# A two-block transformer kernel on one core: five small moves in the order of loads, weight splits and bank emptying

## The reference, cut to what matters

```python
g = jax.nn.sigmoid(gates.reshape(b, s, N_BRANCH, D_MODEL))
merged = g[:, :, 0] * (o_fox @ w_fox_out) + g[:, :, 1] * (o_dsa @ w_dsa_out) + g[:, :, 2] * (o_sb @ w_sb_out)
return merged @ w_out
```

## Time and profile before

| | us |
|---|---|
| median of 3 runs | 2405.51 (2404.97 to 2410.62) |
| profiled execution | 2403.74 |
| its span | 2401.9 |
| TensorE busy | 2264.0 (94%) |
| VectorE busy | 1502.5 (63%) |
| ScalarE busy | 1081.5 (45%) |
| GpSimd busy | 350.4 (15%) |
| mean granted TensorE clock | 0.968 |

### The profile page before, as it was taken

How to read it: one execution, slowest core, us unless ns; L and a number is a source line. 1 busy time by engine, 2 the same in 40 slices (tenths; PEclk the granted TensorE clock), 3 DMA queues, 4 the chain that set the end, 5 groups by cost and what they waited for, 6 DMA issues and landing times.

```text
span 2401.9 us, 40464 instructions
## 1 busy us (share of the span) xinstructions
PE 2264.0 (94%) x17516; PEld 2157.3 (90%) x17516; DVE 1502.5 (63%) x2186; ACT 1081.5 (45%) x1285; POOL 350.4 (15%) x300
## 2 busy tenths in 40 slices
PE   7988899998789999999999899999999999899998
PEld 6878799997679999999998798999999988788998
DVE  5566687843467878667756547667656556556665
ACT  4445544534455445335336355335334236445333
POOL 1680000045000000000535110000000015310000
PEclk9999999998899999999999799999999999989999
DMA  8663255543234554555643344455555643344552
GB/s 244 178 169 105 97 178 200 161 157 106 70 106 168 181 196 159 194 175 175 186 127 109 113 162 155 162 201 173 186 177 176 161 146 108 106 158 132 181 203 91
DMA packets 314660, 374.28 MB, mean 156 GB/s; under 512 B 23127, under 2 KB 280931, under 8 KB 313331
## 3 DMA queue, kind: packets, MB, share of 16 engines
q1 hardware_dynamic: 309283, 353.83, 45.5%
q0 software_dynamic: 3424, 11.50, 1.7%
q10 hardware_dynamic: 1776, 6.37, 0.8%
HBM read 362.49 MB, written 9.18 MB: 155 GB/s over the span
## 4 chain that ended last, share of the span: by engine, by line
PE 83%; DVE 9%; ACT 5%; issue 2%; POOL 0%; DMA 0%; ACTq 0%; DVEq 0%
PE banks L857 23%; PE banks L860 22%; PE banks L858 22%; PE banks L885 3%; PE banks L886 3%; PE banks L889 3%; DVE wlo L1752 2%; ACT whi L1335 2%; PE banks L1113 1%; PE banks L1151 1%; PE banks L1137 1%; PE banks L1033 1%; PE banks L1020 1%; DVE x_lo L1810 1%; PE banks L867 1%
## 5 line engine op out<-in xcount | busy, mean ns | idle before, releaser
L857 PE MATMUL banks<-x_hi,wlo 128*128 128x256 f32 (+1 forms) x4344 | 1110.0, 288 | 39.7 <-DVE wlo L1752 15.4
L858 PE MATMUL banks<-x_lo,whi 128*128 128x256 f32 (+1 forms) x4344 | 1098.5, 285 | 0.0
L1335 ACT ACTIVATE whi<-raw 128x2048 fp32r<-128x2048 f32 (+1 forms) x340 | 637.3, 1878 | 680.0 <-PE banks L860 617.6
L857 PEld LDWEIGHTS banks<-x_hi,wlo 128*128 128x128 f32 (+1 forms) x4344 | 843.6, 194 | 60.5 <-issue 34.2
L858 PEld LDWEIGHTS banks<-x_lo,whi 128*128 128x128 f32 (+1 forms) x4344 | 844.5, 194 | 1.0 <-issue 1.0
L1752 DVE TENSOR_TENSOR wlo<-raw,whi 128x2048 fp32r<-128x2048 f32 (+2 forms) x292 | 658.3, 2264 | 170.7 <-ACT whi L1335 170.4
L860 PE MATMUL banks<-x_hi,whi 128*128 128x256 f32 x4344 | 691.9, 285 | 0.0
L860 PEld LDWEIGHTS banks<-x_hi,whi 128*128 128x128 f32 x4344 | 599.6, 194 | 3.6 <-issue 0.9
L825 POOL TENSOR_TENSOR wlo<-raw,whi 128x512 fp32r<-128x512 f32 x184 | 239.7, 1340 | 1173.9 <-ACT whi L1335 1173.9
L885 PE MATMUL banks<-x_hi,wlo 128*128 128x256 f32 (+1 forms) x632 | 177.1, 312 | 31.5 <-DVE gt L1786 11.6
L886 PE MATMUL banks<-x_lo,whi 128*128 128x256 f32 (+1 forms) x632 | 169.1, 299 | 0.0
(11 more groups left out here) (254 smaller groups left out, 1966.3 us busy)
## 6 DMA issues: line engine op xcount, KB each, us to landing
raw<-in_ffn_w_gu SPq DMA_DIRECT2D x88, 1024.0 KB, 5.2
raw<-in_ffn_w_down SPq DMA_DIRECT2D x66, 1024.0 KB, 5.1
raw<-in_ffn_w_up SPq DMA_DIRECT2D x44, 1024.0 KB, 5.1
raw<-in_w_in SPq DMA_DIRECT2D x42, 1024.0 KB, 5.3
raw<-in_ca_w_kv SPq DMA_DIRECT2D x16, 1024.0 KB, 5.3
raw<-in_od_w_in SPq DMA_DIRECT2D x12, 1024.0 KB, 5.1
raw<-in_ev_w_in SPq DMA_DIRECT2D x10, 1024.0 KB, 6.2
raw<-in_w_in SPq DMA_DIRECT2D x20, 512.0 KB, 5.1
```

Of the source, the lines that this page charges most:

```text
L857: eng.matmul(out, a[1], b[0], start=first and i == 0, stop=False, skip_group_check=True)
L858: eng.matmul(out, a[0], b[1], start=False, stop=False, skip_group_check=True)
L1335: eng.activation(whi[s % SETS][:, 0:ch["n"]], raw[i % SLOTS][:, 0:ch["n"]], ACT.Copy).then_inc(S["weights_hi"], 1)
```

## The change

- x is loaded by SyncE's queue ahead of chunk 0, no longer by ScalarE's.
- The memory chunks of the first block are split by VectorE in one instruction, no longer by GpSimd in four.
- In slot 10 of the hybrid attention, VectorE empties banks up to `end` instead of up to M2, so M2 and M3 are emptied at the head of that slot.
- In a `linear` stage the split goes up to the second chunk ahead that is not a memory chunk (`two_on`). This differs only where a memory chunk lies among the next two: at the two query units of the cross-attention in the second block.
- In the FFN with convolution, steps 0 and 1 split one chunk more behind the taps: chunk 4 in step 0 and chunk 6 in step 1.

```diff
+        def two_on(c):
+            for _ in range(2):
+                c += 1
+                while c < len(chunks) and chunks[c]["mem"] is not None:
+                    c += 1
+            return c
...
-            c = mem_chunk(layer, buf, last_unit, pool=True)
+            c = mem_chunk(layer, buf, last_unit)
...
-                            6: (G[9], F[2]), 7: (G[10], G[9]), 8: (M[0], G[10]), 9: (M[2], M[0]), 10: (end, M[2])},
+                            6: (G[9], F[2]), 7: (G[10], G[9]), 8: (M[0], G[10]), 9: (M[2], M[0]), 10: (end, end)},
...
# SyncE, ahead of load(0); taken out of ScalarE's start()
+            eng.dma_start(rows_in, io["x"][0].rearrange("(t p) c -> p t c", p=P)).then_inc(S["x_loaded"], 16)
...
# linear(), on ScalarE and on VectorE
-                    split_upto(un["chunk"] + 2)
+                    split_upto(two_on(un["chunk"]))
...
# ffn() with convolution, on ScalarE and on VectorE, behind the taps
-                        if j >= FF_LAG:
-                            split_upto(st["steps"][j - FF_LAG]["down"][0] + 2)
+                        split_upto(st["steps"][j - FF_LAG]["down"][0] + 2 if j >= FF_LAG else st["steps"][j]["val"][0] + 3)
```

More of the change, by code:

```diff
@@ L1395, in start @@
             def start(st):
-                eng.dma_start(rows_in, io["x"][0].rearrange("(t p) c -> p t c", p=P)).then_inc(S["x_loaded"], 16)
                 eng.dma_start(con[:, 0:n_early], io["consts"][:, 0:n_early]).then_inc(S["consts_loaded"], 16)
```

## The result

The changed kernel takes 2380.18 us, median of 4 runs (2379.33 to 2381.45); the kernel before took 2405.77 beside it. The ratio is 0.9896, 95% interval 0.9880 to 0.9913: 25.6 us faster, where 30.5 were forecast. The profiled execution took 2381.45 us, 22.3 less than the one of before.

What follows compares the result with a forecast made beforehand. TensorE holds 83% of the chain of waits, so time falls only where it stands still or its clock is low. Parts A to E less new clock falls sum to 30.5 us: 2375.0 on the median, range 2361.5 to 2391.5.

Steps and rivals of the forecast that it cites:

- A: Kernel start: x loaded ahead of chunk 0 on SyncE's queue gains 0.8 us, ends -1.0 and +2.0.
- B, mLSTM layer: First layer's memory split on VectorE: 3.0 us wait goes, one of 5 us comes one step on; -0.5 us.
- B, second layer: Second layer's memory split on VectorE: key chunk 0 starts 3.2 us earlier, plus 1.7 us of low clock taken back.
- The rule of the lock: Both layers: two-input VectorE and GpSimd instructions exclude each other; by it 0.4 us less each, 2.8 for 3.2 in the second.
- C: Slot 10, both hybrid layers: M2 and M3 emptied before the split gains 14.1 us, 7.6 and 6.5.
- D: Second block's cross-attention: key chunk 0 split before the norm gains 4.4 us of waits and 3.4 of clock.
- E: Convolution FFNs, both layers: chunks 4 and 6 split behind the taps gain 3.4 and 2.0 us, together 5.4.
- new falls: mLSTM and both FFNs: low clock behind the new waits costs 2.0 us against the sum, end 5.1.
- The mean clock: Whole kernel: a sign of the forecast, mean granted clock up from 0.968 to about 0.972.
- Rivals 2 to 5: 2: no falls, 2362, 0.12; 3: merged attention gains nothing, 2389, 0.06; 4: slower, 2416, 0.04; 5: waits return, 2403, 0.04.
- rival 1: Edited places: waits go, clock stays low and falls once more in each FFN; 17.9 us gained, 2387.6; chance 0.20.

Runs made afterwards that it cites:

- second profile: The changed kernel run once more with nothing edited; 2378.32 us, ratio 0.9883 to the kernel before.
- the kernel without E: The changed kernel with chunks 4 and 6 of both convolution FFNs split at the head of the next step again; 2381.91 us, ratio 0.9897.
- both holds: Changed kernel, mLSTM key chunk 1 split on VectorE, GpSimd held until head 0's, then head 1's probabilities; 2369.96 us, ratio 0.9850 to the kernel before.

## Why the prediction was right or wrong, point by point

- **A** was sized at 0.8 and is 0.5 by the profiles, 0 by the medians. The steady start came at 21.14, not at 20.6. The 0.3 us that VectorE lost to late copies of x is gained: ScalarE is done with chunk 0 at 13.05 in both profiles, and VectorE begins at 13.08, not at 13.39. But ScalarE gets chunk 0 no sooner (11.14, and 11.13 before), so the rest of the 0.8 did not come. With x back on ScalarE's queue that loss was 0.5, but chunk 0 came 0.25 sooner (10.89), which left nothing of A.
- **B, mLSTM layer.** This step failed, and by my own mark (a loss over 3 us) I was wrong here: -0.5 was forecast and -4.8 measured. The mechanism was right: the 3.26 us wait went, a new one of 5.79 (4 to 6 said) came one step on, because the probabilities run beside GpSimd. The price was too small. I let TensorE come out 0.5 us late; at full clock it is 2.4. Of this 1.0 is there when the scores of head 2 start (20.97 us behind those of head 0 in the second profile, 19.99 before), and 1.4 comes behind them, since the new wait brings 3.4 us of low clock (0.57 in 162 to 170; before, 1.7 us in 154 to 160, where TensorE had slack). The rest of the 4.8 was a fall at the head of the stage, which comes and goes in one and the same program.
- **B, second layer.** TensorE gains 3.2 us over the stage, as forecast, but only 2.8 of it at the wait: from the last long wait ahead of it (561.85, and 567.98 after) it is 11.9 us before and 9.1 after. The other 0.4 comes in the matmuls behind, for which the forecast gave no reason. The 1.7 of clock did not come: low clock costs 5.2 us in 568 to 582 (0.63) in both profiles.
- **The rule of the lock.** The Trainium skill, "SBUF — State Buffer", section "SBUF: two separate sides", by which the gain is 2.8 and not 3.2, came out at 2.8: GpSimd's first piece behind VectorE's memory split took 1.57 us in this layer and 1.68 in the other, where its pieces take 1.3 otherwise. It also says that the holder keeps the port pair for a whole instruction; the trace agrees: VectorE's two-input 4-column steps between the probabilities take 1.1 us beside GpSimd and 0.16 without, and a piece of GpSimd's split takes 1.3.
- **C** was forecast at 14.1 and is 15.0 (13.3 undone): 8.5 for 7.6 and 6.5 for 6.5. M2 and M3 are emptied ahead of the split, output 8 gates (1.06 us), w_out keeps two waits (1.26 and 1.28 us in the first layer, 1.27 and 0.97 in the second).
- **D** was forecast at 7.8 and is 8.4 (8.1 undone), the waits 0.66 where 0.6 was said.
- **E** was forecast at 5.4 less 2.0 of clock and is 2.9 by the two profiles, 1.4 against the kernel without E. Chunk 4 has no wait; chunks 6 and 8 wait 1.6 and 1.9. What failed is the reckoning of the fall: I set 2.0 us for new falls in three places; the two of the FFNs alone cost 1.6 each, where the falls of the kernel without E had been hidden in a wait. The waits themselves were sized well: without a fall the two layers gain 3.7 and 2.2, 5.9 for 5.4.
- **Falls elsewhere** cost 2.9 us net in places that nothing touches. I had no term for it; the changed kernel's second profile divides them otherwise. That the sum of it all came out only 4.9 off by the medians is in part luck.

The mean clock is 0.969, not 0.972. Rivals 2 to 5 did not happen; rival 1's condition, the clock as low as before, held in the first block and not in the second. In sum, by the profiles: B is 6.0 us short, E 0.5, A 0.3, untouched places 2.9; C and D are 1.5 over; 8.2 in all, of 30.5. The medians give 3 of these back; at which places, no run shows.

What stays open: what makes the clock fall at the head of the mLSTM in one execution and not in another.

## What to carry to other kernels

Before moving work off GpSimd, look at which VectorE instructions run beside what GpSimd does next: here the wait of 5.8 us came from that collision, and holding GpSimd for the length of two short VectorE phases, with one chunk's split moved between them, gained 10 us, more than moving the memory split, which is worth nothing to the medians. A fall of the clock costs only where TensorE is what ends last. In the FFN it cost nothing ahead of a place where TensorE had to wait anyway, and 1.6 us behind the last such place: a wait that can't be removed is better put ahead. And price a part by undoing it alone, since two profiles of one program differ by 2.6 us in one stage.

## What the runs showed of the hardware

- Beside GpSimd's splits VectorE's steps of 128x4 with two inputs took 1.1 to 1.2 us and not 0.16, the two 128x256 products with a column 2.4 and not 0.62, the two multiply-adds 2.8 and not 0.88. Those that read a bank took 0.41 and 0.42, and the reciprocal of 128x4, with one input, 0.18 in both cases.
- It goes the other way as well. In the kernel with both holds, GpSimd's first piece met VectorE's split of key chunk 1 (the first row) and took 3.28 us instead of 1.3, so that its four pieces (the second row) took 7.06 instead of 5.1:

```profile
155.19 2.28 DVE L1764 TENSOR_TENSOR wlo<-raw,whi 128x2048 fp32r<-128x2048 f32 x1
...
155.35 7.06 POOL L837 TENSOR_TENSOR wlo<-raw,whi 128x512 fp32r<-128x512 f32 x4 [5.59 <-DVE wk L2206]
```

- At the head of the mLSTM the clock fell in 6 of the 13 profiles of kernels with the change or parts of it, and did not in 7; the changed kernel and the same kernel again are of one program and one of each kind. The 30 us at 0.54 in the first hybrid layer came in both kernels with the 4.3 us wait there and in none without. The same wait in the second hybrid layer of the kernel before was followed by 0.66 over 10 us only the earlier trace rows.
